# The Down projection for two token blocks at once, as a two by two block product in Strassen's form

## The reference, cut to what matters

```
x  = x + mix @ w_out                       # mix: 2048 x 1024, from the attention
h2 = rmsnorm(x, norm_ffn_g)
x  = x + (silu(h2 @ w_gate) * (h2 @ w_up)) @ w_down     # w_down: 2816 x 1024
return rmsnorm(x, final_norm_g)
```

## Time and profile before

| what | us |
|---|---|
| median of 3 runs (lowest, highest) | 3078.14 (3071.31, 3078.14) |
| the profiled execution, its time | 3077.6 |
| its span in the trace | 3075.8 |
| TensorE busy | 3001.3 |
| VectorE busy | 1962.3 |
| ScalarE busy | 1610.4 |
| GpSimd busy | 781.6 |

### The profile page before, as it was taken

One profiled execution on the slowest core, in us unless ns is written; L12 is line 12 of the kernel. 1 busy time (PEld: TensorE's weight loads), 2 busy tenths in 40 slices (PEclk: granted clock), 3 DMA queues, 4 the chain that ended last, 5 costly groups with the idle time before them and its releaser, 6 DMA issues.

```text
span 3075.8 us, 52440 instructions
## 1 busy us (share of the span) xinstructions
PE 3001.3 (98%) x19328; PEld 2671.5 (87%) x19328; DVE 1962.3 (64%) x2906; ACT 1610.4 (52%) x2716; POOL 781.6 (25%) x847
## 2 busy tenths in 40 slices
PE   7999999999999999999999999999999999999998
PEld 6887778777777999999889998999889998899987
DVE  6224430077666777787567766887648876488754
ACT  5122211167777888887555544555445554365543
POOL 1922221055665877777200000000000000000000
PEclk9999999999999999999999999999999999999999
DMA  5488894556643540411436642566425664246642
GB/s 191 129 212 197 186 220 107 131 130 144 145 107 74 112 105 6 110 52 39 134 105 185 184 153 92 168 210 184 158 89 159 211 184 168 93 146 211 183 127 72
DMA packets 236031, 431.48 MB, mean 140 GB/s; under 512 B 23568, under 2 KB 61712, under 8 KB 235024
## 3 DMA queue, kind: packets, MB, share of 16 engines
q1 hardware_dynamic: 217968, 382.43, 42.6%
q0 software_dynamic: 17600, 46.15, 7.9%
q10 hardware_dynamic: 288, 0.59, 0.1%
HBM read 370.35 MB, written 104.86 MB: 155 GB/s over the span
## 4 chain that ended last, share of the span: by engine, by line
PE 64%; DVE 7%; POOL 5%; ACT 3%; issue 1%; DVEq 0%; ACTq 0%; POOLq 0%
PE f_ps L2127 28%; PE f_ps L2028 21%; PE h_o L974 6%; PE h_t L960 3%; PE h_z L696 2%; PE h_z L699 2%; DVE h_negmax L1094 2%; POOL h_more L1258 2%; POOL h_work L1258 2%; DVE h_more L1210 2%; DVE h_more L1126 2%; ACT h_work L993 1%; ACT h_more L993 1%; POOL h_srstd L1303 1%; PE f_ps L2061 0%
## 5 line engine op out<-in xcount | busy, mean ns | idle before, releaser
L1591 ACT ACTIVATE f_whi<-f_wraw 128x512 fp32r<-128x512 f32 x856 | 535.6, 627 | 434.9 <-PE f_ps L2127 301.0
L1598 DVE TENSOR_TENSOR f_wlo<-f_wraw,f_whi 128x512 fp32r<-128x512 f32 x856 | 590.5, 690 | 260.3 <-ACT f_whi L1591 258.2
L2127 PE MATMUL f_ps<-f_hi_s,f_whi 128*128 128x256 f32 x1408 | 397.1, 282 | 0.5 <-DVE f_up L1897 0.5
L2127 PE MATMUL f_ps<-f_lo_s,f_whi 128*128 128x256 f32 x1408 | 397.2, 282 | 0.0
L2127 PE MATMUL f_ps<-f_hi_s,f_wlo 128*128 128x256 f32 x1408 | 396.9, 282 | 0.0
L1298 POOL TENSOR_TENSOR h_work<-h_work,h_more 128x1024 f32<-128x1024 f32 (+3 forms) x192 | 302.5, 1588 | 110.1 <-DVE h_more L1210 97.3
L1568 POOL TENSOR_TENSOR f_rstd<-f_var,f_exponent 128x4 f32<-128x4 f32 x7 | 7.1, 1008 | 1235.2 <-DVE f_var L1814 1235.2
L2127 PE MATMUL f_ps<-f_lo_a,f_whi 128*128 128x256 f32 x1056 | 297.8, 282 | 0.0
L2127 PE MATMUL f_ps<-f_hi_a,f_whi 128*128 128x256 f32 x1056 | 297.5, 282 | 0.0
L2127 PE MATMUL f_ps<-f_hi_a,f_wlo 128*128 128x256 f32 x1056 | 297.4, 282 | 0.0
L2028 PE MATMUL f_ps<-f_whi,f_shi 128*128 128x512 f32 x696 | 273.4, 393 | 0.0
(11 more groups left out here) (196 smaller groups left out, 6931.0 us busy)
## 6 DMA issues: line engine op xcount, KB each, us to landing
f_wraw<-in_w_stream SPq DMA_DIRECT2D x504, 256.0 KB, 2.7
f_wraw<-sums_scratch SPq DMA_DIRECT2D x352, 256.0 KB, 2.9
sums_scratch<-in_w_stream POOLq DMA_DIRECT2D x132, 256.0 KB, 5.3
qk_scratch<-p_ohi SPq DMA_DIRECT2D x64, 256.0 KB, 3.3
qk_scratch<-p_olo SPq DMA_DIRECT2D x64, 256.0 KB, 5.1
h_k<-qk_scratch SPq DMA_DIRECT2D x32, 512.0 KB, 9.6
h_qmain<-qk_scratch SPq DMA_DIRECT2D x64, 256.0 KB, 13.2
h_qmain<-qk_scratch SPq DMA_DIRECT2D x32, 448.0 KB, 11.1
```

What stands on the lines that cost most here:

```text
L1591: act.activation(w_hi[ring][:], w_raw[ring][:], ACT.Copy).then_inc(S["hi_split"], 1)
L1598: dve.tensor_tensor(w_lo[ring][:], w_raw[ring][:], w_hi[ring][:].bitcast(F32), ALU.subtract).then_inc(S["lo_split"], 1)
L2127: mm = pe.matmul(outs[i], w[ring][:, col], a[name][:, c, :], start=(c == 0 and m == 0), stop=(c == 3 and m == 2))
```

## The change

Down is done for two blocks (a pair, q = 0 or 1) at once. The activations of the pair are a two by two matrix of blocks: rows are the two token blocks, columns the two halves of the 22 tiles (11 each). The weights are two by two as well: the two halves of the tiles by the two halves of the model width. The block product is made of 7 products of 11 units each, with the operands a11, s1, s2, s3, s4, a12, a22 of `DOWN`, where s1 = a21 - a22, s2 = a11 - s1, s3 = a21 - a11, s4 = a12 - s2.

Its parts:

- The four sums of Down's weights are made in DRAM by 88 more DMAs of GpSimd (`down_sum_step`), behind its second norm of the last part.
- The activations no longer stay in SBUF. VectorE writes each tile to one of two slots, and SP stores it to DRAM (`store_act`, 88 stores of 256 KB).
- In Down SP loads for each unit one piece of activations, or two for s1 to s4 (`load_pieces`), into 3 slots. VectorE subtracts the second from the first (`stage`), for s1 and s2 SP stores the difference to DRAM (`store_kept`), since later products use it.
- SP's program is now one list: load the weights of unit U, then whatever follows unit U-14 (`follow`).
- Each product is added to the parts of x it belongs to as soon as it is made (`add_product`). The first one is also copied to a running total by ScalarE.
- x of all four blocks stays in SBUF, and the output of blocks 0 and 1 is stored during the last gate_up, that of block 2 at the end.
- The order of the parts is new (`SEGMENTS`).
- In the input projection two semaphores of the loads of x are shared; the DMAs are the same.

```diff
+def down_sum_step(pool, w_stream, sums_dram, sums_stored, n):
+    def part_of(part, r):
+        v = part // 2 * (FT // 2) + r
+        return w_stream[KC + 2 * FT + part % 2 * (FT // 2) + v // 2, :, v % 2 * GROUP:(v % 2 + 1) * GROUP]
+    add_parts(pool, sums_dram, sums_stored, n, FT // 2, part_of)
...
+DOWN = ["a11", "s1", "s2", "s3", "s4", "a12", "a22"]
+SUMMED = range(1, 5)
...
+SEGMENTS = [("out", 0, 0, OUT_UNITS), ("out", 1, 0, OUT_UNITS), ("gate", 0, 0, GATE_UNITS), ("out", 2, 0, OUT_UNITS),
+            ("gate", 1, 0, GATE_UNITS), ("down", 0, 0, 3 * RUN), ("out", 3, 0, OUT_UNITS), ("down", 0, 3 * RUN, 2 * RUN),
+            ("gate", 2, 0, GATE_UNITS), ("down", 0, 5 * RUN, 2 * RUN), ("gate", 3, 0, GATE_UNITS), ("down", 1, 0, DOWN_UNITS)]
...
+def product_bank(q, p):
+    return 4 * ((p + 1 - q) % 2)
...
+            def load_unit(u):
+                if u == gate_unit(0):
+                    for done, count in sums_stored:
+                        sp.wait_ge(done, count)
+                if u == down_unit(0, 0):
+                    for done, count in down_stored:
+                        sp.wait_ge(done, count)
+                sp.wait_ge(S["lo_split"], u - RING + 1)
+                sp.dma_start(w_raw[u % RING][:], source(u)).then_inc(w_loaded[u % RING], 16)
+            def store_act(b, f):
+                sp.wait_ge(S["act_made"], FT * b + f + 1)
+                sp.dma_start(act_dram[b, f], act_out[f % 2][:]).then_inc(act_stored[f % 2], 16)
...
+            def load_pieces(q, n):
+                g = stage_of(q, n)
+                p, r = divmod(n, RUN)
+                if n in (0, RUN):
+                    b = 2 * q + (n == RUN)
+                    for s in range(2):
+                        sp.wait_ge(act_stored[s], acts_through(b, RUN - 1))
+                if g >= STAGES:
+                    sp.wait_ge(S["stage_lo"], g - STAGES + 1)
+                    if n >= STAGES and kept(n - STAGES):
+                        sp.wait_ge(act_stored[g % STAGES], kept_through(q, n - STAGES))
+                cells = {"a11": act_dram[2 * q, r], "a12": act_dram[2 * q, RUN + r], "a21": act_dram[2 * q + 1, r],
+                         "a22": act_dram[2 * q + 1, RUN + r], "s1": kept_dram[q, 0, r], "s2": kept_dram[q, 1, r]}
+                one, two = {"a11": ("a11", None), "s1": ("a21", "a22"), "s2": ("a11", "s1"), "s3": ("a21", "a11"),
+                            "s4": ("a12", "s2"), "a12": ("a12", None), "a22": ("a22", None)}[DOWN[p]]
+                sp.dma_start(piece[g % STAGES][:], cells[one]).then_inc(pieces_loaded[g % STAGES], 16)
+                if two is not None:
+                    sp.dma_start(other[g % STAGES][:], cells[two]).then_inc(pieces_loaded[g % STAGES], 16)
+            def store_kept(q, n):
+                g = stage_of(q, n)
+                p, r = divmod(n, RUN)
+                sp.wait_ge(S["act_sums"], summed_through(q, n))
+                sp.dma_start(kept_dram[q, p - 1, r], piece[g % STAGES][:]).then_inc(act_stored[g % STAGES], 16)
...
+            def follow_down(q, n):
+                if n == 0 or (q, n) == (0, 5 * RUN):
+                    store_act(2 * q + 1 if n == 0 else 2, FT - 1)
+                if (q, n) == (0, 1):
+                    sp.wait_ge(S["act_made"], 2 * FT)
+                    sp.dma_start(natural[:], mix_blocks[3]).then_inc(S["mix_loaded"], 16)
+                if n + STAGES < DOWN_UNITS and kept(n + STAGES):
+                    store_kept(q, n + STAGES)
+                if n + 5 < DOWN_UNITS:
+                    load_pieces(q, n + 5)
...
+            for u in range(RING + 8, TOTAL + 2 * RING):
+                if u < TOTAL:
+                    load_unit(u)
+                follow(u - 2 * RING)
+            store_block(last - 1)
+            store_block(last)
+            sp.wait_ge(S["stored"], 16 * BLOCKS * TPB)
...
+            power(0, 1)
+            for n in range(SUM_OPS * (RUN + 1)):
+                down_sum_step(pool, w_stream, down_sums, [done for done, _ in down_stored], n)
+            power(0, 2)
+            power(0, 3)
...
# ScalarE
+            def stage(q, n):
+                g = stage_of(q, n)
+                if n // RUN in SUMMED:
+                    act.wait_ge(S["act_sums"], summed_through(q, n))
+                else:
+                    act.wait_ge(pieces_loaded[g % STAGES], pieces_through(q, n))
+                if g >= STAGES:
+                    act.wait_ge(S["multiplied"], stage_unit(g - STAGES) + 1)
+                act.activation(stage_hi[g % STAGES][:], piece[g % STAGES][:], ACT.Copy).then_inc(S["stage_hi"], 1)
...
+            def add_product(q, p, t):
+                made = bank[product_bank(q, p) + t][:]
+                if p < PRODUCTS - 1 or q < last_pair:
+                    dve.wait_ge(S["multiplied"], down_unit(q, (p + 1) * RUN - 1) + 1)
+                cleared = 16 * q + 4 * p + t + 1
+                if p == 0:
+                    dve.wait_ge(S["copied"], 4 * q + t + 1)
+                    dve.tensor_tensor(place(q, 0, 0, t), made, place(q, 0, 0, t), ALU.add).then_inc(S["cleared"], 1)
+                elif p == 1:
+                    dve.tensor_tensor(place(q, 0, 1, t), made, place(q, 0, 1, t), ALU.add)
+                    dve.tensor_tensor(place(q, 1, 1, t), made, place(q, 1, 1, t), ALU.add).then_inc(S["cleared"], 1)
+                elif p == 2:
+                    dve.tensor_tensor(total[:, t, :], made, total[:, t, :], ALU.subtract).then_inc(S["cleared"], 1)
+                    dve.wait_ge(S["cleared"], cleared)
+                    dve.tensor_tensor(place(q, 0, 1, t), total[:, t, :], place(q, 0, 1, t), ALU.add)
+                elif p == 3:
+                    dve.tensor_tensor(total[:, t, :], made, total[:, t, :], ALU.add).then_inc(S["cleared"], 1)
+                    dve.wait_ge(S["cleared"], cleared)
+                    dve.tensor_tensor(place(q, 1, 0, t), place(q, 1, 0, t), total[:, t, :], ALU.subtract)
+                    dve.tensor_tensor(place(q, 1, 1, t), total[:, t, :], place(q, 1, 1, t), ALU.add).then_inc(S["x2_half"], 1)
+                else:
+                    odd, half = {4: (0, 1), 5: (0, 0), 6: (1, 0)}[p]
+                    dve.tensor_tensor(place(q, odd, half, t), made, place(q, odd, half, t), ALU.add).then_inc(S["x2_half"], 1)
...
+            def stage(q, n):
+                g = stage_of(q, n)
+                s = g % STAGES
+                if n // RUN in SUMMED:
+                    dve.wait_ge(pieces_loaded[s], pieces_through(q, n))
+                    dve.tensor_tensor(piece[s][:], piece[s][:], other[s][:], ALU.subtract).then_inc(S["act_sums"], 1)
+                dve.wait_ge(S["stage_hi"], g + 1)
+                dve.tensor_tensor(stage_lo[s][:], piece[s][:], stage_hi[s][:].bitcast(F32), ALU.subtract).then_inc(S["stage_lo"], 1)
...
+            def down(q, p):
+                for k in range(RUN):
+                    n = p * RUN + k
+                    u = down_unit(q, n)
+                    if k < TPB and p and down_unit(q, p * RUN) == down_unit(q, p * RUN - 1) + 1:
+                        add_product(q, p - 1, k)
+                    if (q, p, k) == (0, 3, 0):
...
+                    if n + STAGES < DOWN_UNITS:
+                        stage(q, n + STAGES)
                     if u + RING < TOTAL:
                         plain_lo(dve, u + RING)
...
+            gate_up(0)
+            project(2)
+            gate_up(1)
+            for p in range(3):
+                down(0, p)
+            project(3)
+            down(0, 3)
+            down(0, 4)
+            gate_up(2)
+            down(0, 5)
+            down(0, 6)
+            gate_up(3)
+            for p in range(PRODUCTS):
...
+                down(1, p)
```

More of the change, by code:

```diff
@@ L1401, in ahead_buffers @@
     operands = small + 8 * TPB * 8 + 4 * KC
[L1402 to L1406, removed]
+    third_x = operands + PRODUCTS * 2 * row
+    ring_rest = third_x + TPB * row
+    stage = ring_rest + (RING - 2) * 2 * half
+    pieces = stage + STAGES * row
+    fourth_x = pieces + STAGES * half
+    others = fourth_x + TPB * row
+    second_x = others + STAGES * half
+    junk = second_x + TPB * row
+    assert junk + half <= H["base"] and stage + 2 * 4 * KC * BLK <= others
+    F = dict(x_in=at("xin", [P, TPB, D_MODEL], keys), junk=at("junk", [P, HALF], junk),
              natural=at("natural", [P, TPB, D_MODEL], low), g_ffn=at("gffn", [P, KC], small),
@@ L1527, in sync @@
-            sp.dma_start(natural[:, :, MIX_AHEAD:D_MODEL], mix_blocks[1][:, :, MIX_AHEAD:D_MODEL]).then_inc(S["mix_loaded"], 16)
[L1528 to L1532, removed]
-            for sem_of, count in sums_stored:
-                sp.wait_ge(sem_of, count)
-            down = OUT_ITEMS + 2 * FT
@@ L1849, in side_sum @@
                     dve.wait_ge(S["dve_plain"], 4 * b + 2)
-                    one, other = side_cells("a21"), side_cells("a11")
+                    one, two = side_cells("a21"), side_cells("a11")
                 elif name == "s1":
```

(21 more changed lines are left out.)

677 lines of the change are left out of this document (409 added, 268 removed).

## The result

The changed kernel takes 3131.54 us (median of 4 runs, 3129.94 to 3134.47) beside 3074.74 us of the kernel before (4 runs, 3071.31 to 3078.14): **ratio 1.0186 [1.0168, 1.0203], 57 us slower**. Forecast were 3103 us and "slower".

A forecast was written before the change was run, and what follows sets the result against it. TensorE was taken to bound the kernel before, late pieces the changed Down. On 3077.6 us, -60.4 + 77.0 - 12.3 + 5.7 + 15.3 = +25.3 gave 3103 us, range 3045 to 3165.

The forecast's parts named there:

- the pace of 2.75: TensorE's time in us for one Down unit of 12 matmuls; a11, a12 and a22 were forecast to hold it.
- GpSimd's sums at nothing: GpSimd's 88 DMAs for the sums of Down's weights, made ahead of Down, were forecast to cost nothing.
- The fall of the clock: In Down, a granted clock of 0.91 makes a unit 3.0 us, under the step times, so costs nothing more.
- The rate rival: In Down, the DMA rate decides, not landing: 300 GB/s, s1 and s2 need 3.50 us per unit; 3057 us, chance 0.10.
- the never-late rival: Down's pieces are never late; only s4 of pair 0 is too much for VectorE: 3029 us, chance 0.08.
- A, the landing of the last piece: In Down, from VectorE's step end to that landing: 3.4, 4.15, 4.9 us for two, three, four transfers; +77.0 us.
- The run of seven: Rival in Down: pieces land as in a run of seven loads, s1 to s4 step at 4.3 and 4.7; 3181 us, chance 0.13.
- Other adds, 0.61 to 1.22 per step, fit in the wait: VectorE's adds of products in Down, outside the s4 bursts, were forecast to hide in its wait for data.
- 4.1 us of delay are free at the start of each pair: Slack at Down's start in each pair, and once more behind the output projection in pair 0: -12.3 us.
- The 2 MB load: Mix for block 3, issued in pair 0's first product ahead of a piece: 11.2 us where two steps are 5.5, +5.7.
- the s4 bursts: VectorE's adds of s3 in s4's first four steps, in pair 0 also block 2's preparations: +15.3 us over both pairs.
- the tail keeps its shape: The kernel's end was forecast to stay as before, at no cost.

The follow-up runs named there:

- experiment 1: Changed kernel with the pieces and what else follows a unit issued one VectorE step earlier against the weight loads: 3075.91 us, ratio 0.9995.
- experiment 4: Changed kernel without GpSimd's 88 DMAs for the sums of Down's weights: 3132.13 us, ratio 1.0183.
- experiments 2 and 6: On the changed kernel: 2 leaves out the stores of s1's and s2's differences, 3110.73 us; 6 issues the weight load behind store and pieces, 3099.89 us.
- experiments 5 and 11: Mix for block 3 loaded as four loads in place of one: 5 on the changed kernel, 3136.85 us; 11 on that of Experiment 10, 3059.78 us.
- Experiment 10: On experiment 1, VectorE adds the previous product behind the difference of the pieces, not ahead of it: 3060.16 us, ratio 0.994.
- experiment 7: Changed kernel with the differences of the pieces for s1 to s4 moved from VectorE to GpSimd: 3143.89 us, ratio 1.0223.
- experiment 8: Kernel of experiment 1 with the differences of the pieces for s1 to s4 moved from VectorE to GpSimd: 3074.66 us, ratio 0.9997.

## Why the prediction was right in sign and short in size

**Right, and shown.** The mechanism: pieces asked for one step ahead make a round from SP's issue to VectorE's step end, longer than two units of TensorE. The chain shows each of its links, and one step of lead gives back 56 us (experiment 1). s1 and s2 are the slowest, s3 and s4 next, a12 and a22 keep the pace of 2.75. GpSimd's sums at nothing (experiment 4, 0.6 us). Gate-and-up keeps its speed. The fall of the clock costs nothing more at the place followed above. The rate rival is refuted for this kernel by experiment 1's 289 GB/s, the never-late rival by TensorE's gaps.

**Where it was short**, by its own terms:

- *A, the landing of the last piece, "the first lands 2.65 behind E, and each further 256 KB adds its own transfer time"*, taken as 0.75: this is the step that failed. Pair 1's s1 and s2 took 4.20 and 4.14 us per step, not 3.81; s3 3.73, not 3.44. Turned back through (A + 2.72)/2, A was 5.7 and 5.6 for four transfers and 4.7 for three, where I took 4.9 and 4.15; read from the trace, over the steps of pair 1 that waited for a piece, the medians are 5.6 and 4.7. So each further 256 KB added about 1.0 us, not 0.75. The price of a transfer ahead in the queue is in experiments 2 and 6: 1.2 us for a store, 0.5 to 1.0 for a weight load. In pair 1 this is 22 x (4.17 - 3.81) = 7.9 us for s1 and s2 and 2.8 for s3 and s4 (s4's adds came out 0.4 cheaper than forecast). The run of seven, my high end, gave 5.9 and 6.7: the truth is between, nearer to what I took.
- *"Other adds, 0.61 to 1.22 per step, fit in the wait"*: not in s3. By the prediction's own numbers the wait hides 0.83, and two adds take 1.22, so 4 x 0.39 us per pair are missing from its sum. In pair 1 four steps of s3 took 3.92 us, in experiment 1 as well: VectorE's time, not a landing. They are 1.9 of the 3.2 us by which s3 was short.
- *"4.1 us of delay are free at the start of each pair"*: not behind a gate-and-up stage. SP had spent its lead on activations that are ready only as the stage ends. The pieces of the opening were issued at 2848.34, 0.35 us behind the stage's end, and landed 4.89 later (the chain's first row above). The operand of unit 3 was ready at 2854.6 and wanted at 2856.2, 1.6 us of slack; and the first eight steps of a11, forecast at the pace, were 3.07 us each. In pair 1 that is some 5 us.
- *Pair 0*, forecast 47.3, lost 51.2: here two misses cancel in part, by luck. The first three products lost 30.9 where 24.9 were forecast (steps of 4.17 and 4.27 in s1 and s2, A again), s3 and s4 20.0 where 22.4 were. The 2 MB load (two steps of 11.45 us where 11.2 were forecast) and the s4 bursts (5.65 to 5.92 where 1.83 + 1.22 + 2.61 = 5.66) were sized about right. Splitting the load gave nothing back (experiments 5 and 11), so the mention of it as a cost of its own holds only as a share of delay that is there anyway.
- *"At nothing: ... the tail keeps its shape", gate-and-up untouched*: 4.9 us together in truth, spread over the openings and the tail; no experiment took them apart.

Sum of the misses: pair 1 56.6 - 38.4 = 18.2 (7.9 + 2.8 + 5 + 2.5 that stay unassigned), pair 0 3.9, the rest 4.9: 27.0, which is 52.3 - 25.3. Some 15 of it go to A: the 7.9 and 0.9 of the 2.8 in pair 1, and the 6.0 of the first three products of pair 0. (The transfer times 0.82 and 0.65 of the prediction are 0.84 and 0.67 for 262144 bytes; 0.75 lies between either way.)

The Trainium skill's 341 GB/s for 1 MB (DMA: Bandwidth & Descriptors, Bandwidth), which by itself spoke for a loss in s1 and s2, isn't what made it: a step there took 4.2 us, 250 GB/s, and 3.36 us in experiment 1, 312 GB/s, with the same bytes. The traces don't set 341 as a ceiling: the kernel before had 405 GB/s over 8 us. Experiment 10 comes near the figure, 331 GB/s at a share of 0.98, and there a loss through rate, as the page's estimate has it, may be part of what is left.

**What stays open.** Experiment 10 gains 18 of the 60.4 us removed. Down still loses 33 of the others: its four stretches take 104.0, 75.4, 64.0 and 222.7 us there, 466.1 where 432.8 would be the pace. That is 10.3 us in s4 of pair 0, where nearly every step also prepares block 2's operands, some 6 in s1 and s2 of pair 1, where the DMA engines are nearly full, and the rest in smaller parts. (TensorE's waits on the low part add up to 17.6 us only; ends of matmuls are modelled in these rows, and may hide a part of each wait.) Some 10 us more lie outside Down, in the openings of gate-and-up and in the tail, and weren't taken apart.

## What to carry to other kernels

Before counting instructions saved, draw the round of a load: from the event that frees the queue (here the last split of a step) over everything issued ahead of it, to its landing and its user, and divide by the steps of lead. With one step of lead, a lookahead of seven on the weights helps nobody else; one step more was worth more here (56 us) than any byte taken away (21 and 31). Once loads come in time, look at the share of the DMA engines stage by stage: the mean over pair 1 in experiment 1 is 0.74, over its s1 and s2 alone (2854 to 2926 us) 0.92. Give every 256 KB transfer that stands ahead in the same queue 0.5 to 1.2 us, as measured here, and put those with slack last, but never a store whose landing a later load waits for.

## What the runs showed of the hardware

GpSimd's difference of two 128x512 f32 tiles took 1.42 us (1.30 in experiment 7) where VectorE's takes 0.69; I had expected 0.8. The Trainium skill, GPSIMD Engine Reference, Elementwise — side-by-side cycle accounting, puts GpSimd at about twice VectorE's time for operations on two inputs: the trace agrees.

Worse, VectorE stands still beside it when its operation comes second. The two timelines of experiment 8, GpSimd's first, then VectorE's:

```profile
2957.41 1.30 POOL L1748 TENSOR_TENSOR f_piece<-f_piece,f_other 128x512 f32<-128x512 f32 x1 [0.23 <-DMA f_other<-kept_scratch]
2960.22 1.39 POOL L1748 TENSOR_TENSOR f_piece<-f_piece,f_other 128x512 f32<-128x512 f32 x1 [1.51 <-DMA f_other<-kept_scratch]
```

```profile
2957.87 1.38 DVE L2136 TENSOR_TENSOR f_slo<-f_piece,f_shi 128x512 fp32r<-128x512 f32 x1 [1.84 <-ACT f_shi L1845]
2959.17 0.68 DVE L1783 TENSOR_TENSOR f_wlo<-f_wraw,f_whi 128x512 fp32r<-128x512 f32 x1
2959.77 0.68 DVE L2136 TENSOR_TENSOR f_slo<-f_piece,f_shi 128x512 fp32r<-128x512 f32 x1
2960.38 1.78 DVE L1783 TENSOR_TENSOR f_wlo<-f_wraw,f_whi 128x512 fp32r<-128x512 f32 x1
```

GpSimd's two operations end at 2958.71 and 2961.61. The two of VectorE that begin under them take 1.38 and 1.78 us and end at 2959.25 and 2962.16, both 0.55 behind GpSimd's end; the other two take 0.68, one beside no GpSimd operation, one begun before GpSimd's. The long ones look as if they had begun only once GpSimd was done. It isn't these two alone: of 24 splits on VectorE that begin under a difference of GpSimd in experiment 8, 23 end 0.55 us behind it. The Trainium skill, SBUF — State Buffer, Terms, says just that: the two engines share one port pair, one holds it for its whole instruction, and the other fully blocks. The trace agrees.

The landing of a 256 KB load in Down depended on what was issued ahead of it. Of pair 1's first half, 2848 to 2985 us (issues, KB, median us from issue to landing):

```profile
f_piece<-act_scratch SPq DMA_DIRECT2D x36, 256.0 KB, 3.6
f_wraw<-down_sums SPq DMA_DIRECT2D x33, 256.0 KB, 3.1
kept_scratch<-f_piece SPq DMA_DIRECT2D x22, 256.0 KB, 3.4
f_other<-act_scratch SPq DMA_DIRECT2D x17, 256.0 KB, 4.2
```

3.1 for the first of a step, 4.2 for the last, at a mean DMA share of 0.74, where a lone one took 2.7.
